# One level of a blocked triangular inverse taken off TensorE in a hybrid DeltaNet and attention layer

## The reference, cut to what matters

```python
kb = kc * bc[..., None]
l_mat = einsum('nbhid,nbhjd->nbhij', kb, kc) * decay_strict
rhs = concatenate([vc * bc[..., None], kb * exp(gcum)[..., None]], axis=-1)
sol = lax.linalg.triangular_solve(eye + l_mat, rhs, left_side=True, lower=True, unit_diagonal=True)
def step(s, xs):                      # a scan over the chunks, forward and backward
    v_new = u_n - w_n @ s
    o_n = qd_n @ s + a_n @ v_new
    s = s * gl_n + kd_n^T @ v_new
```

## Time and profile before

| | |
|---|---|
| median of 3 runs | 2080.33 us (2075.86 to 2085.59) |
| the profiled execution's own time | 2080.7 us |
| its span, first to last instruction | 2078.9 us |
| TensorE busy in the span | 1971.5 us (95%) |
| VectorE, ScalarE, GpSimd busy | 895.7 (43%), 623.3 (30%), 238.1 us (11%) |
| mean granted TensorE clock | 0.987 |

### The profile page before, as it was taken

How to read it: one execution, slowest core, us unless ns; L and a number is a source line. 1 busy time by engine, 2 the same in 40 slices (tenths; PEclk the granted TensorE clock), 3 DMA queues, 4 the chain that set the end, 5 groups by cost and what they waited for, 6 DMA issues and landing times.

```text
span 2078.9 us, 39482 instructions
## 1 busy us (share of the span) xinstructions
PE 1971.5 (95%) x17462; PEld 1527.1 (73%) x17462; DVE 895.7 (43%) x1765; ACT 623.3 (30%) x1061; POOL 238.1 (11%) x392
## 2 busy tenths in 40 slices
PE   5779999999999999999999999999999888999997
PEld 2138888888777777777787877866787566788885
DVE  1324344465334455544555554531135644454332
ACT  4313222223132333233222323432235333322211
POOL 0000000000022222211111222011000100320000
PEclk9799999999999999999999999999999999999999
DMA  8872222223232222222222224566433222373332
GB/s 309 273 241 63 58 61 56 59 79 86 61 92 63 63 73 63 62 63 68 68 63 62 57 68 114 189 213 219 155 93 100 82 81 91 114 271 118 115 123 80
DMA packets 158628, 227.19 MB, mean 109 GB/s; under 512 B 10145, under 2 KB 108698, under 8 KB 157178
## 3 DMA queue, kind: packets, MB, share of 16 engines
q1 hardware_dynamic: 136265, 156.09, 25.2%
q0 software_dynamic: 14416, 54.42, 7.9%
q10 hardware_dynamic: 7776, 14.16, 1.9%
HBM read 202.10 MB, written 22.54 MB: 108 GB/s over the span
## 4 chain that ended last, share of the span: by engine, by line
PE 83%; DMA 6%; ACT 5%; DVE 3%; issue 2%; POOL 1%; SPq 0%; ACTq 0%; POOLq 0%; DVEq 0%
PE psum L1378 22%; PE psum L1380 20%; PE psum L1379 20%; DMA w_raw_mod<-w_mod_dram 4%; PE psum L1669 2%; PE psum L1445 2%; PE psum L1441 2%; PE psum L1516 1%; ACT inv L654 1%; PE psum L1453 1%; DVE w_lo L892 1%; PE psum L1408 1%; ACT w_hi L588 1%; PE psum L1472 1%; DMA w_raw<-w_in_dram 1%
## 5 line engine op out<-in xcount | busy, mean ns | idle before, releaser
L892 DVE TENSOR_TENSOR w_lo<-w_raw,w_hi 128x1024 fp32r<-128x1024 f32 x232 | 290.6, 1253 | 652.3 <-ACT w_hi L588 651.9
L588 ACT ACTIVATE w_hi<-w_raw 128x1024 fp32r<-128x1024 f32 x232 | 245.7, 1059 | 1004.1 <-PE psum L1380 959.4
L1378 PE MATMUL psum<-h_hi,w_hi 128*128 128x512 f32 x1152 | 482.4, 419 | 4.7 <-DVE w_lo L892 2.5
L1380 PE MATMUL psum<-h_hi,w_lo 128*128 128x512 f32 x1152 | 453.0, 393 | 0.0
L1379 PE MATMUL psum<-h_lo,w_hi 128*128 128x512 f32 x1152 | 452.6, 393 | 0.0
L1378 PEld LDWEIGHTS psum<-h_hi,w_hi 128*128 128x128 f32 x1152 | 216.8, 188 | 59.6 <-issue 13.8
L1380 PEld LDWEIGHTS psum<-h_hi,w_lo 128*128 128x128 f32 x1152 | 216.8, 188 | 50.2
L1379 PEld LDWEIGHTS psum<-h_lo,w_hi 128*128 128x128 f32 x1152 | 217.6, 189 | 31.9
L962 DVE SCALAR_TENSOR_TENSOR conv_acc<-conv_in,convw,conv_acc 128x772 f32<-128x772 f32 x96 | 98.2, 1023 | 3.4
L1378 PE MATMUL psum<-w_hi,m_hi 128*128 128x512 f32 x256 | 99.6, 389 | 0.0
L1379 PE MATMUL psum<-w_lo,m_hi 128*128 128x512 f32 x256 | 99.6, 389 | 0.0
(11 more groups left out here) (310 smaller groups left out, 2909.0 us busy)
## 6 DMA issues: line engine op xcount, KB each, us to landing
w_raw<-w_in_dram SPq DMA_DIRECT2D x168, 512.0 KB, 3.8
w_raw_mod<-w_mod_dram SPq DMA_DIRECT2D x64, 512.0 KB, 5.7
w_raw_modg<-w_mod_dram POOLq DMA_DIRECT2D x32, 512.0 KB, 5.1
w_raw<-w_out_dram SPq DMA_DIRECT2D x32, 512.0 KB, 3.7
gate_scratch<-gate_stage ACTq DMA_DIRECT2D x48, 256.0 KB, 4.3
w_raw<-w_proj_a_dram SPq DMA_DIRECT2D x16, 512.0 KB, 3.9
w_raw<-w_proj_b_dram SPq DMA_DIRECT2D x16, 512.0 KB, 3.6
gates<-gate_scratch POOLq DMA_DIRECT2D x32, 256.0 KB, 4.3
```

Of the source, the lines that this page charges most:

```text
L588: act.activation(part(whi[i % 2], p), part(place, p), ACT.Copy).then_inc(S("w_hi"), 1)
L892: dve.tensor_tensor(part(wlo[i % 2], p), part(raw_of(n)[0], p), part(whi[i % 2], p).bitcast(f32), ALU.subtract).then_inc(S("w_lo"), 1)
L1378: pe.matmul(out_ap, lh, rh, start=first, stop=False, skip_group_check=shared)
L1380: return pe.matmul(out_ap, ll, rh, start=False, stop=last, skip_group_check=shared)
```

## The change

The slot `couple` 0 disappears from every pair, with its 32 matmuls: 244 slots instead of 256. In its place ScalarE, as soon as VectorE has written L for a direction, copies the four diagonal blocks of 32 rows into `XC` (four instructions per direction), and VectorE, after it has worked off the slot ahead of `couple` 1, multiplies by a mask, subtracts from the identity and transposes into `YC`, for direction 0 and then 1. TensorE's `couple` 1 waits for that with two new semaphores, `pairs0` and `pairs1`. In context pairs 1 to 3, `gram` now stands ahead of `ks` instead of behind it. All later slots move up by one per pair, so their q changes.

```diff
-            kinds = [("decay", 0)] + [("ks", 0)] * early + [("gram", 0)] + [("qk", 0)] * lat
-            for n in range(len(BLOCKS)):
-                kinds += [("couple", n)] + [("correct", n)] * (n > 0)
+            kinds = [("decay", 0)] + [("ks", 0)] * (early and lat) + [("gram", 0)]
+            kinds += [("ks", 0)] * (early and not lat) + [("qk", 0)] * lat
+            for n in range(1, len(BLOCKS)):
+                kinds += [("couple", n), ("correct", n)]
...
+            def gdn_blocks(slot):                                   # ScalarE
+                for d in (0, 1):
+                    act.wait_ge(S(f"gd{d}"), slot["i"] + 1)
+                    for q in range(4):
+                        own = slice(32 * q, 32 * q + 32)
+                        act.activation(XC[d][own], LL[d][own, :, own], ACT.Copy).then_inc(S(f"blocks{d}"), 1)
...
                     if s and (s["kind"] in ON_SCALAR or (s["kind"] == "correct" and s["n"] == len(BLOCKS) - 1)):
                         gdn(s)
+                    if s and s["kind"] == "gram":
+                        gdn_blocks(s)
...
+            def pair_blocks(pair):                                  # VectorE
+                for d in (0, 1):
+                    m = PAIR2 + 32 * (1 - d)
+                    mask = consts[:, m:m + 32].unsqueeze(1).to_broadcast([P, 4, 32])
+                    eye = consts[:, EYE32:EYE32 + 32].unsqueeze(1).to_broadcast([P, 4, 32])
+                    dve.wait_ge(S(f"blocks{d}"), 4 * (pair + 1))
+                    ln(dve.tensor_tensor(XC[d][:], XC[d][:], mask, ALU.mult))
+                    ln(dve.tensor_tensor(XC[d][:], eye, XC[d][:], ALU.subtract))
+                    dve.transpose(YC[d][:].rearrange("p u n -> p (u n)"), XC[d][:].rearrange("p u n -> p (u n)")).then_inc(
+                        S(f"pairs{d}"), 1)
...
-                        if n == 0:
-                            mask = consts[:, PAIR2 + 32 * d:PAIR2 + 32 * d + 32].unsqueeze(1).to_broadcast([P, 4, 32])
-                            eye = consts[:, EYE32:EYE32 + 32].unsqueeze(1).to_broadcast([P, 4, 32])
-                            ln(dve.tensor_tensor(YC[d][:], bank4(b, 32), mask, ALU.mult))
-                            ln(dve.tensor_tensor(YC[d][:], eye, YC[d][:], ALU.subtract))
-                            flip_blocks(d).then_inc(done, 1)
-                            continue
...
                     if s and s["kind"] not in ON_SCALAR:
                         gdn(s)
+                        if SLOTS[s["i"] + 1:] and SLOTS[s["i"] + 1]["kind"] == "couple" and SLOTS[s["i"] + 1]["n"] == 1:
+                            pair_blocks(s["pair"])
...
+                    if k == "couple" and n == 1:                    # TensorE
+                        pe.wait_ge(S(f"pairs{d}"), slot["pair"] + 1)
...
-                                if n == 0:
-                                    ins = pe.matmul(bank4(b, 32)[own, u, :], lhs, ident[own, own], start=True, stop=True)
-                                    continue
```

## The result

The changed kernel took 2083.02 us as the median of 20 runs (2080.84 to 2091.31), the kernel before 2079.65 in as many runs on the same chips. The ratio is 1.0022, with a 95% interval from 1.0012 to 1.0032: slower by 2.5 to 6.7 us, which is real and small. The forecast was 2087, its range 2077 to 2097.

The account below looks back on a forecast made before the run. TensorE was taken to bound the scan's stage. Slots gone (-10.9), a wait gone (-0.9), new waits (+21.0), clock (+2.6) and shifted slots (-5.0) gave +6.8 us, so 2087 us, range 2077 to 2097.

Parts of the forecast that it names:

- TensorE bounds, in order: In the scan's stage TensorE sets the time, busy 658.3 of 673 us, and takes its work in order.
- Slots that go, 10.9 us: Twelve `couple` 0 slots leave TensorE while their k-steps stay; 0.91 us each, 10.9 us saved.
- New waits, 21.0 us: TensorE waits ahead of `couple` 1 for the first inverse: latent pairs 7.4 us, context pairs and pair 0 the rest.
- The clock, 2.6 us: TensorE's clock falls to half behind the long waits of pairs 1 and 3, costing 2.6 us together.
- two falls of twice the length: Bound on the clock term: two falls lasting twice as long, 2.6 us more.
- the rival of twelve falls: The clock falls behind every new wait, twelve times instead of two: 13 us more, 2100 us, 10% chance.
- The shift of slots, 5.0 us: Pairs begin at q = 0 or 2, so slots late behind q = 3 (`ks`, `gram`, `qs`) recover 5.0 us.
- The three pieces of gates that no longer carry slots run at the bare pitch.: Behind the last slot, three gate pieces freed of slots cost only bare k-steps, already counted in the 10.9 us.
- Nothing else late behind the waits.: Behind TensorE's new waits no other work comes late; `lo_part` after `qk` runs inside the following k-step.
- The rival of a hidden inverse: The first inverse is hidden behind other work, so 16.8 us go: 2063.5 us, 5% chance.
- that of dear copies: ScalarE's 32-partition copies take 0.62 us each instead of 0.31: 2098 us, slower, 9% chance.
- that pairs 1 and 3 have slack: Long waits of context pairs 1 and 3 don't arise, the high part being early: 8.3 us less, 2079, 15% chance.

Follow-up runs that it names:

- e6: Changed kernel with two k-steps without a slot per pair, one ahead of `couple` 1, one ahead of `kt` (or `z`): 2046.31 us, ratio 0.9857.
- e12: Changed kernel with `ks` ahead of `gram` again in context pairs 1 to 3, second run of this version: 2079.88 us, ratio 1.0006.
- e8: Changed kernel with the gate modulation started three positions later (`N_MODG0 = N_FIN + 14` for 11): 2080.09 us, ratio 1.0007.
- e11: The changed kernel run once more, with nothing altered: 2083.84 us, ratio 1.0027 to the kernel before.
- e1: Changed kernel with ScalarE's high part ahead of its eight copies where `gram` stands at q = 3: 2077.43 us, ratio 0.9993.
- e5: Kernel before the change with one k-step without a slot per pair, behind `kt` (or `z` in the two last pairs): 2057.82 us, ratio 0.9916.
- e3: Kernel before the change with one k-step without a slot per pair, ahead of `kt` (or `z`): 2053.01 us, ratio 0.9876.

## Why the prediction was right, step by step

- **TensorE bounds, in order.** Right. Every wait that came on TensorE is in the time, and VectorE's and ScalarE's shares said nothing about it.
- **Slots that go, 10.9 us.** Right: 0.91 us a slot, seen in e6, where nothing waits in its place.
- **New waits, 21.0 us.** Measured by the same rows: latent pairs 0.93 each, the forecast's own number (7.4); pair 2, 1.7 for 1.6; pairs 1 and 3, 3.99 and 0.55 each, 4.54 for 4.45; pair 0, 1.53 and 0.98, 2.5 for 3.1. Together 20.7. TensorE in pair 0:

```profile
616.96 0.44 PE L1458 MATMUL psum<-inv32T,L 32*32 32x16 f32 x32 [1.38 <-DVE inv32T L1000]
618.28 0.44 PE L1458 MATMUL psum<-inv32T,L 32*32 32x16 f32 x32 [0.88 <-DVE inv32T L1000]
```

  Pair 0 was over-priced since the trace before had a late L there. VectorE's L, before and after:

```profile
617.49 2.37 DVE L993 SCALAR_TENSOR_TENSOR L<-psum,crow,decay 128x128 f32<-128x128 f32 x8 [3.35 <-POOL decay L480]
```
```profile
613.36 2.16 DVE L1016 SCALAR_TENSOR_TENSOR L<-psum,crow,decay 128x128 f32<-128x128 f32 x8 [2.19 <-PE psum L1428]
```

  Before, it waited for GpSimd's mask of the decays and was ready 4.61 us after `gram` started (615.25 to 619.86); in this profile of the changed kernel it was ready 3.25 us after (612.27 to 615.52). In e12 it waited for GpSimd again, and TensorE stood for 2.51 and 0.88 us in pair 0, close to the forecast. So this term hangs on the execution, and that it came out lower was luck.

- **The clock, 2.6 us.** Under-sized by half: 5.1. The falls at 3.83 us lasted 6.8 us, not the 3.5 of the earlier trace rows, and took 1.86 us each; pair 0, for which none was forecast, had one of 3.5 us behind idle times of 1.38 and 0.88, worth 1.4 us. The bound (two falls of twice the length) held for pairs 1 and 3. In latent pairs it stayed at full speed, so the rival of twelve falls is false. (e8 has one fall in latent pair 4, behind a stall of 1.24 us on top of the usual two waits.) The rule of the Trainium skill ("TensorE: Matmul & The Clock Gate", Part 1), that the clock goes to half after idleness, agrees with the falls in pairs 0, 1 and 3. It doesn't say that every wait costs a fall, and those of 0.37 and 0.41 us in the latent pairs cost none.
- **The shift of slots, 5.0 us.** Under-sized: 7.1. `ks` and `gram` gave 4.6 for the 4.4 forecast, output slots 1.3 for 0.6, and 1.3 came from small stalls at `decay`, `couple` 1 and `couple` 6 that I had not listed.
- **"The three pieces of gates that no longer carry slots run at the bare pitch."** This step was wrong: +3.4 us. What fills those pieces, the modulation's visits, is spread by a rule that the change moves (e8).
- **Nothing else late behind the waits.** Right. What else went, 3.0 us net, is what the other terms leave over. It is of the size of the stalls that hang on no wait of the program; the one at 901.69 with its fall of the clock is as much by itself. They are not all chance: many move from profile to profile, but `correct` 4 of pair 6 has 0.6 to 0.9 us in all eight profiles with 244 slots and no gap. Their cause stays open.

Sum by the measured terms: -10.9 - 0.9 + 20.7 + 5.1 - 7.1 - 3.0 + 3.4 = +7.3, against 7.1 in the trace and +6.8 forecast. So the total is better than its parts, by luck: two misses upward (the clock 2.5, the visits 3.4) and two downward (the shift 2.1, the stalls 3.0) cancel. The 7.1 us rest on one profile of the kernel before. By the medians the change costs 3.4 us, with an interval of 2.5 to 6.7, and 4.6 when the same kernel ran again (e11); the forecast of 6.8 lies just above that interval. Of the 4 us between 2087 and 2083.02, 0.7 are that the kernel before took 2079.65 us beside it and not 2080.33; why the medians show less than the stretch stays open. That a measurement can hardly tell less than 0.5% was wrong: with 20 runs each it told 0.22%. The rival of a hidden inverse is false in the change as made and nearly true with gaps (e6); that of dear copies is false (a pitch of 0.33 us, 2.63 for eight); that pairs 1 and 3 have slack is false; that they could have been given it, by one swap, is e1.

## What to carry to other kernels

Work taken off the bounding engine is worth only what its replacement doesn't make that engine wait for: lay the new chain out from source to use, in each engine's program order, and count what of the bounding engine's work stands between them; a gap or a swap ahead of the use can be worth more than the work removed. Where small work rides in slots of a fixed frame (here four to a piece), look first at whether its period is a multiple of the frame: one idle position per pair took 0.8% off the kernel before (e5), and 1.2% where it also covered a wait (e3), more than twice what the slots removed here were worth. And a rule that spreads later work over "what is left" belongs in the sum.

## What the runs showed of the hardware that I had not expected

- Eight copies of 32 partitions by 128 elements take ScalarE 2.63 us; eight scalings of 128 partitions by as many elements take 2.46. A quarter of the partitions saved nothing, and four copies, to move one block of each quarter, cost four.
- Behind the wait of 2.18 us for ScalarE the clock stayed at 1.00 in the kernel before. Behind the same wait of 2.18 us in the changed kernel it was 0.54 from 602.50 to 606.00. An idle time of this length may cost a fall or not, in the same program place. All fourteen profiles have this wait of 2.18 us, and nine have a fall of the clock behind it.

```profile
602.50:606.00 3.50, 3.50 (x10) 2.77 (x9) 0.01 (x1) 0.81 (x2) 3.09 (x5) 0.54 1.01 299
```

- The transpose of a 128x128 tile by blocks of 32 takes VectorE 0.31 us, and the masks at 0.25 to 0.29 us cost from SBUF what they cost from PSUM.
